# Differential attention block in float32: mask of the scores by VectorE, all modulation rows on TensorE, products begun among them, loads of q and of the output weights moved up

## What is computed

```python
mod = silu(c) @ ada_w + ada_b
shift, scale, gate = split(mod, 3)
h = rms_norm(x, norm_pre) * (1 + scale) + shift
q, k, v, z = (h @ w_in[:, i*2048:(i+1)*2048] for i in range(4))
# per block of 128 queries and head; map m of q, k is [.., m, :]
sc = einsum('qmd,kmd->mqk', q, k) * 128 ** -0.5
mask = key_chunk <= q_chunk                      # chunks of 64
p = softmax(where(mask, sc, -1e30))
attn = p[0] - lam * p[1]
o = rms_norm(attn @ v, subln) * (1 - 0.2) * silu(z)
out = x + gate * rms_norm(o @ w_out, norm_post)
```

## Time and profile before

| | |
|---|---|
| median of 3 runs | 2067.22 us (2063.76 to 2068.3) |
| profiled execution | 2068.47 us |
| its span, first to last instruction | 2066.7 us |
| mean granted TensorE clock | 0.985 |
| TensorE busy | 1981.3 us, 96% |
| VectorE busy | 1295.6 us, 63% |
| ScalarE busy | 785.1 us, 38% |
| GpSimd busy | 580.9 us, 28% |

### The profile page before, as it was taken

How to read it: one execution, slowest core, us unless ns; L and a number is a source line. 1 busy time by engine, 2 the same in 40 slices (tenths; PEclk the granted TensorE clock), 3 DMA queues, 4 the chain that set the end, 5 groups by cost and what they waited for, 6 DMA issues and landing times.

```text
span 2066.7 us, 26660 instructions
## 1 busy us (share of the span) xinstructions
PE 1981.3 (96%) x9324; PEld 1610.8 (78%) x9324; DVE 1295.6 (63%) x1988; ACT 785.1 (38%) x1567; POOL 580.9 (28%) x640
## 2 busy tenths in 40 slices
PE   3689999999999989999999999999999989999998
PEld 1168888888888878788888888888888878888886
DVE  3766676666566436777777777777777745434343
ACT  4333333333454323344444444444444333322240
POOL 2333233233456224232332333233232210000000
PEclk9889999999999999999999999999999999999999
DMA  9657666663556586776758676676767685476552
GB/s 311 198 183 244 221 199 207 200 197 124 175 183 227 211 325 219 207 236 195 233 178 248 196 216 216 209 236 200 234 193 237 196 275 165 123 229 199 178 153 82
DMA packets 391489, 426.52 MB, mean 206 GB/s; under 512 B 21078, under 2 KB 287420, under 8 KB 388796
## 3 DMA queue, kind: packets, MB, share of 16 engines
q1 hardware_dynamic: 391072, 424.76, 65.1%
q10 hardware_dynamic: 284, 0.05, 0.0%
HBM read 294.70 MB, written 130.03 MB: 206 GB/s over the span
## 4 chain that ended last, share of the span: by engine, by line
PE 90%; DMA 2%; DVE 2%; issue 2%; POOL 1%; ACT 1%; SPq 1%; DVEq 0%; POOLq 0%; ACTq 0%
PE ps L1561 28%; PE ps L1563 27%; PE ps L1562 27%; PE ps L1667 2%; PE ps L1675 2%; PE ps L1645 1%; DVE acc L1146 1%; PE ps L1541 1%; SPq L475 1%; PE ps L1694 1%; POOL sums L727 1%; POOL stg L747 1%; DMA h_dr<-stg 1%; DVE blk L1175 0%; DMA w_raw<-in_diff_w_out_dram 0%
## 5 line engine op out<-in xcount | busy, mean ns | idle before, releaser
L1561 PE MATMUL ps<-blk,ring 128*128 128x512 f32 x1536 | 612.4, 399 | 12.6 <-POOL blk L738 5.9
L1563 PE MATMUL ps<-blk,ring 128*128 128x512 f32 x1536 | 600.9, 391 | 0.0
L1562 PE MATMUL ps<-blk,ring 128*128 128x512 f32 x1536 | 600.4, 391 | 0.0
L1561 PEld LDWEIGHTS ps<-blk,ring 128*128 128x128 f32 x1536 | 289.7, 189 | 73.1 <-issue 12.1
L1563 PEld LDWEIGHTS ps<-blk,ring 128*128 128x128 f32 x1536 | 289.5, 188 | 62.2
L1562 PEld LDWEIGHTS ps<-blk,ring 128*128 128x128 f32 x1536 | 290.1, 189 | 57.2
L1111 DVE TENSOR_TENSOR ring<-sums,ring 128x512 fp32r<-128x512 f32 x256 | 221.1, 864 | 128.8 <-ACT ring L830 125.6
L727 POOL TENSOR_TENSOR sums<-raw 128x512 f32<-128x512 f32 x128 | 192.6, 1505 | 307.5 <-DVE ring L1111 290.4
L830 ACT ACTIVATE ring<-sums 128x512 fp32r<-128x512 f32 x256 | 160.4, 627 | 202.3 <-PE ps L1563 195.8
L1111 DVE TENSOR_TENSOR ring<-raw,ring 128x512 fp32r<-128x512 f32 x192 | 162.0, 845 | 83.0 <-ACT ring L830 82.3
L1432 DVE TENSOR_TENSOR w_lo<-w_raw,w_hi 128x512 fp32r<-128x512 f32 x112 | 77.4, 691 | 191.2 <-ACT w_hi L1026 191.1
(11 more groups left out here) (163 smaller groups left out, 3110.1 us busy)
## 6 DMA issues: line engine op xcount, KB each, us to landing
raw<-in_diff_w_in_dram SPq DMA_DIRECT2D x64, 1024.0 KB, 7.0
d_dr<-cc SPq DMA_DIRECT2D x128, 256.0 KB, 2.7
cc<-d_dr SPq DMA_DIRECT2D x128, 256.0 KB, 3.7
w_raw<-in_diff_w_out_dram SPq DMA_DIRECT2D x128, 256.0 KB, 3.6
ada<-in_ada_w_dram SPq DMA_DIRECT2D x108, 256.0 KB, 4.7
ada<-in_ada_w_dram SPq DMA_DIRECT2D x32, 512.0 KB
q_sb<-q_dr SPq DMA_DIRECT2D x64, 256.0 KB, 3.2
k_sb<-k_dr SPq DMA_DIRECT2D x64, 256.0 KB, 3.8
```

The costliest lines, as they stand in the source:

```text
L1561: MM(dst, a_hi, b_hi, start=start, stop=False, skip_group_check=True)
L1562: MM(dst, a_hi, b_lo, start=False, stop=False, skip_group_check=True)
L1563: return MM(dst, a_lo, b_hi, start=False, stop=stop, skip_group_check=True)
```

## The change

1. The mask matmul goes; VectorE writes -1e30 over the corner (64 queries by 64 keys) of the scores, waits for it (`masked`), and takes the maximum.
2. All eight slots of a chunk are TensorE's; `rows0`, `ada_sum` and `acc0` go. The row and its turned columns share one bank, so that a chunk's first row waits for `mod_ok` of the chunk before. All seven low halves are VectorE's.
3. Products 0, 1 and 3 are begun (`begin`) for j = 0 and 1 behind the third chunk, for j = 2 behind the fourth, before its factors are used; only j = 3 is left for `product`. P5 and P3 of the first group use bank 1.
4. SP: the first weight load stands behind slot 7 instead of 15; the first load of q and k ahead of slot NA + 26; the first four loads of the output weights three products before the end of the products; in the last head q and k of the next block behind the first load of a block. ScalarE splits the first output weight before it squares the last block of head 6.

```diff
+    X_BANK = (3, 5, 6, 7)
-    ON_PE = (1, 4, 6, 7)
+    EARLY_PRODUCTS = (0, 1, 3)
...
         def bank_of(i, pi):
+            if i == 0 and pi in (P5, P3):
+                return 1
...
+        LOWS = (0, 1, 3, 2, 4, 5, 6)
+        def start_low(pi):
+            return LOWS.index((P1, P2, P3, P5, P7, P6, P4).index(pi)) + 1
...
                 if s >= ADA_RING:
-                    sp.wait_ge(*slots_of(s - ADA_RING))
+                    sp.wait_ge(ada_used, s - ADA_RING + 1)
...
                 load_ada_start(s)
-                if s == 15:
+                if s == 7:
                     load_raw(0)
...
             for n in range(NA, NA + PARTS_IN * NP):
+                if n == NA + 26:
+                    load_qk(0, 0)
                 slot(n)
-            load_qk(0, 0)
...
                         slot(n)
                         n += 1
+                        if n == NALL - 3:
+                            for j in range(4):
+                                load_wo(j)
                     if a + 1 == LH * NB:
-                        for j in range(4):
-                            load_wo(j)
                         load_oz_first(1, 0)
...
                     if i == 0:
+                        if qb + 1 < NB:
+                            load_qk(LH, qb + 1)
                         if qb == 0:
                             for pi in (P3, P4):
                                 store(2 * GP - 1, pi)
...
                         load_z(LH, qb)
-                        if qb + 1 < NB:
-                            load_qk(LH, qb + 1)
...
-            for j in range(4):
-                if j == 3:
-                    for which in range(4):
-                        add_w(0, which)
-                for y in range(3):
-                    pool.wait_ge(h_hi, j * NP + y + 1)
...
-                    TTP(dst[:, 1, j], src, dst[:, 0, j].bitcast(F32), ALU.subtract).then_inc(h_lo_p, 1)
+            for which in range(4):
+                add_w(0, which)
...
+                modulate(4 * j)
+                high_h(0)
+                modulate(4 * j + 1)
+                modulate(4 * j + 2)
+                high_h(1)
+                modulate(4 * j + 3)
+                for y in range(2, NP):
+                    high_h(y)
...
+                    if a + 1 == LH * NB:
+                        split_next(-1)
                     square(h - 1, qb)
...
-            def rows0(s):
...
+                low_h(0)
+                block_sums(ch, tA, 0)
+                low_h(1)
+                block_sums(ch, tA, 1)
+                low_h(3)
+                block_sums(ch, tA, 2)
+                low_h(2)
+                low_h(4)
+                block_sums(ch, tA, 3)
+                low_h(5)
+                low_h(6)
...
                 dve.wait_ge(s_done, a * 2 + m + 1)
+                V.memset(ps[0:CHUNK, bank + qb // HT, qb % HT * P + CHUNK:(qb % HT + 1) * P], MASKED).then_inc(masked, 1)
+                dve.wait_ge(masked, a * 2 + m + 1)
                 V.tensor_reduce(out=nmax[:, m:m + 1], in_=ps[:, bank:bank + 2].rearrange("p b n -> p (b n)")[:, 0:n],
...
                 pe.wait_ge(ada0_in[s % ADA_RING], 32 * (s // ADA_RING + 1))
+                if r == 0 and ch:
+                    pe.wait_ge(mod_ok, ch)
...
+            def begin(j):
+
+                for pi in EARLY_PRODUCTS:
+                    if j == 0:
+                        pe.wait_ge(w_ok, pi + 1)
+                    pe.wait_ge(h_lo_d, NP * j + start_low(pi))
+                    three(ps[:, bank_of(0, pi)], ring[:, pi, 0, j], ring[:, pi, 1, j],
+                          slotA[pi][:, 0, j], slotA[pi][:, 1, j], j == 0, False)
+
             for ch in range(4):
-                for r in ON_PE:
-                    if r == ON_PE[-1]:
-                        ada_sum(ch)
+                for r in range(8):
                     ada_rows(8 * ch + r)
-                    if r == ON_PE[1] and ch:
+                    if r == 4 and ch:
                         for q in range(4):
                             x_turn(4 * ch + q)
                 mod_turn(ch)
+                if ch == 2:
+                    begin(0)
+                    begin(1)
+            begin(2)
...
+                if n == NP:
+                    pe.wait_ge(*read_out(0, P3))
                 if i == 0:
-                    if pi in (P1, P2, P3):
-                        pe.wait_ge(h_lo_p, 9 + (P1, P2, P3).index(pi) + 1)
-                    else:
-                        pe.wait_ge(h_lo_d, 12 + (P5, P7, P6, P4).index(pi) + 1)
+                    pe.wait_ge(h_lo_d, 3 * NP + start_low(pi))
...
-                for j in range(KB):
+                for j in range(KB - 1 if n in EARLY_PRODUCTS else 0, KB):
...
-                    own = e == n
-                    last = three(dst, q_sb[:, 2 * m], q_sb[:, 2 * m + 1], k_sb[:, 2 * m, b:e], k_sb[:, 2 * m + 1, b:e], True, not own)
-                    if own:
-                        last = MM(ps[:, bank + b // HALF, e - b - P:e - b], mcol[0:1, :], mrow[0:1, :], start=False, stop=True,
-                                  skip_group_check=True)
+                    last = three(dst, q_sb[:, 2 * m], q_sb[:, 2 * m + 1], k_sb[:, 2 * m, b:e], k_sb[:, 2 * m + 1, b:e], True, True)
```

More of the change, by code:

```diff
@@ L862, in modulate, with high_h @@
                 act.wait_ge(xT_mm, y + 1)
[L863 removed]
+                A(h32[:, q // 2, half * HALF:(half + 1) * HALF], ps[:, X_BANK[q] if js < 4 else VX], ACT.Identity,
                   scale=mod[:, KT + k:KT + k + 1], bias=mod[:, k:k + 1]).then_inc(h_ev, 1)
             for j in range(4):
[L867 to L868 removed]
+                if j in (1, 2):
+                    for m in (2 * j - 2, 2 * j - 1):
                         high_w(m)
[L870 to L876 removed]
+                act.wait_ge(ada_used, 8 * (j + 1))
+                A(mod_row[0:1, :], ps[0:1, SC], ACT.Copy).then_inc(mod_row_ok, 1)
+                def high_h(y):
+                    if y < 3:
+                        act.wait_ge(h_ev, 4 * j + (1, 3, 4)[y])
+                    else:
                         act.wait_ge(h_sum, 4 * j + y - 2)
@@ L981, in before, with split_next @@
                 return divmod(a - 1, NB)
+            def split_next(u):
+                n = u + 1
+                if n < REG:
+                    act.wait_ge(wo_in[POS[n] % 4], (POS[n] // 4 + 1) * 16)
+                    if n < 2:
+                        act.wait_ge(prod, NALL - 1)
+                    else:
+                        act.wait_ge(wo_used, n - 1)
+                    A(w_hi[:, n % 2], w_raw[:, POS[n] % 4], ACT.Copy).then_inc(wo_hi_ok, 1)
+                if REG - KT <= n < REG:
+                    m = n + KT
+                    act.wait_ge(wo_in[POS[m] % 4], (POS[m] // 4 + 1) * 16)
+                    if m == REG:
+                        act.wait_ge(fin, HT)
+                    A(wl_hi[:, m - REG].rearrange("p (a c) -> p a c", c=P), w_raw[:, POS[m] % 4],
+                      ACT.Copy).then_inc(wo_hi_ok, 1)
             for n in range(NA, NA + PARTS_IN * NP):
@@ L1134, in _ @@
                 V.tensor_scalar(x1[:, :, t, :], x1[:, :, t, :], rsx[:, t:t + 1], None, ALU.mult).then_inc(x_sc, 1)
-            def rows0(s):
-                ch, r = divmod(s, 8)
-                dve.wait_ge(ada0_in[s % ADA_RING], 32 * (s // ADA_RING + 1))
-                for m in range(2):
-                    done = 8 * ch + 2 * (r - sum(q < r for q in ON_PE)) + m
-                    g = 2 * r + m
-                    if g == 0:
-                        i = V.tensor_scalar(acc0[:, ch % 2], ada_start(s)[:, m], cact[:, g:g + 1], None, ALU.mult)
-                    else:
-                        dve.wait_ge(row_ok, done)
-                        i = STT(acc0[:, ch % 2], ada_start(s)[:, m], cact[:, g:g + 1], acc0[:, ch % 2], ALU.mult, ALU.add)
-                    i.then_inc(row_ok, 1)
-            for r in range(8):
-                if r not in ON_PE:
-                    rows0(r)
             for ch in range(4):
-                if ch < 3:
-                    rows0(8 * ch + 8)
-                if ch == 3:
-                    for m in range(LOOK):
+                if ch in (1, 2):
+                    for m in (2 * ch - 2, 2 * ch - 1):
                         low_w(m)
@@ L1530, in x_turn @@
                 for t in range(HT):
[L1531 removed]
+                    i = TR(ps[:, X_BANK[q] if js < 4 else VX, t * P:(t + 1) * P], src[:, k, half * HT + t], ident[:, :])
                 i.then_inc(xT_mm, 1)
```

111 lines of the change are left out of this document (28 added, 83 removed).

## The result

| | before | after |
|---|---|---|
| median of 4 runs, us | 2067.76 (2063.76 to 2071.16) | 2009.06 (2007.15 to 2010.03) |
| profiled execution, us / its span | 2068.47 / 2066.7 | 2007.15 / 2005.2 |
| ratio, 95% interval | | 0.9723 (0.9704 to 0.9742) |

The change saves 58.7 us by the medians, 61.3 by the profiled executions; forecast were 68, a time of 2000. The direction is right and the size is short by nine: the measured median lies at the upper end of the range (1992 to 2010), and by the ratio (0.9723 x 2067.22) it is 2010.0. Where it went is read from the starts of the 64 turns of prob, which cut the program into stretches.

What follows compares the result with a forecast made beforehand. TensorE, busy for 96% of the span, was taken as the bound; 49.3 - 1 + 5.3 + 2 + 3 + 9.5 = 68.1 us off 2068.5 gave 2000.4, said as 2000. Its own range was 1993 to 2008, with four rivals 1992 to 2010.

Steps and rivals of the forecast that it cites:

- A mask matmul costs 0.44 us of TensorE: In the gapless heads, each of 112 mask matmuls removed saves 0.44 us of TensorE, 49.3 us in all.
- The lower bound, 0.25: Gapless heads: each mask saves only its own slot, 0.25 us (28 us in all); as a rival 2021, chance 0.06.
- The write costs 0.30 with its wait: VectorE's write of the masked corner, done 128 times, takes 0.30 us including the wait for it.
- It comes out 0.13 short; seven heads give 1 us back.: Block 3's turn of prob: margin of 0.37 us falls 0.13 short, so TensorE waits; 1 us lost over seven heads.
- the first rival: VectorE late at more turns, its steps twice as long beside POOL: half a microsecond more in some blocks, 2009; chance 0.12.
- The start, -2: Start, all row matmuls on TensorE and products begun early: product 3 ends at 128.1 instead of 130.0, 2 us gained.
- the rival on the clock: Start: TensorE's clock falls at each chunk, four falls costing 2.2 us each, 2009; chance 0.07.
- q and k of the first block, -3: Before the first scores: earlier loads remove 1.25 us of TensorE idle and 1.7 of slow clock, 3 us.
- The last head's first ticks, -9.5: Start of the last head: earlier output weight and q, k loads recover 9.5 of 3.7 + 6.4 = 10.1 us.
- late again, by other names: Rival on the moved loads: they are late again, all 12.5 us of their gain stay unsaved, 2012.5; chance 0.09.
- Last head's masks, 5.3: Last head: eight masks of map 0 and four of map 1 count, 12 x 0.44 = 5.3 us saved.

Runs made afterwards that it cites:

- e9: Changed kernel with GpSimd's three additions of block 3 put ahead of its factor of block 2: 2006.49 us, ratio 0.9707 to the kernel before.
- e2: Changed kernel with the mask left out altogether, neither VectorE's write nor a matmul: 2008.58 us, ratio 0.9726 to the kernel before.
- second execution: Second profiled execution of the same changed kernel, unaltered, from a later run: span 2008.0 us, that run's median 2011.33 us.
- e6: Changed kernel with the mod rows of chunk 1 summed in another PSUM bank: 2005.59 us, ratio 0.9706 to the kernel before.
- e10: Changed kernel with the edits of e6, e8 and e9, and ScalarE copying product 0 out ahead of its last high half of h: 2000.87 us.
- e4: Changed kernel with the moved loads put back at three places of SP's program: 2018.00 us, ratio 0.9774 to the kernel before.
- e8: Changed kernel with the 1 MB load of low halves put behind the first four output weight loads: 2008.06 us, ratio 0.9719 to the kernel before.
- e1: Kernel before with only the mask moved from TensorE to VectorE: 2019.06 us, ratio 0.9776 to the kernel before.

## Why the prediction was right or wrong

- **A mask matmul costs 0.44 us of TensorE.** Right. In the two heads of e9 in which TensorE waits for nothing, a head is 110.26 and 110.32, 7.0 to 7.1 under the shortest two before (117.29 and 117.36), and 16 x 0.44 is 7.04. The lower bound, 0.25, would have left heads of 113.4. The margins around the mask go with it, and the change of bank, which stayed, is not their cause. The Trainium skill, "TensorEngine Tiling (Array Packing)", Key Properties, says that a change of tiling mode drains TensorE; whether a one-row weight is such a change no run here shows, and the cause of the margins stays open.
- **The write costs 0.30 with its wait.** Too high, it is 0.15, and on the path almost nothing (e2).
- **"It comes out 0.13 short; seven heads give 1 us back."** This step failed, one of the two that make up most of what is missing. The prediction measured VectorE's lateness against the product behind the scores, and took the mask to leave that chain 0.5 us less margin. In block 3 the chain does not come from the scores: it runs from the weighted sum of block 2 over ScalarE's square and GpSimd's factor to three additions and prob, and both masks lay beside it, between the same weighted sum and the turn on TensorE. So all of 2 x 0.44 was lost to it: 0.37 - 0.88 = -0.51, and the wait is 0.49. By the shortest heads of e9 it costs 0.75 a head, 5.3 us instead of 1. e9 removes the wait in every head; its trace gets 2.2 us of the 5.3 back, since the load of cc is late next in five heads.
- **VectorE's steps are twice as long beside GpSimd** stood in the first rival, as a reason why other blocks might be late, with 2009 and a chance of 0.12. The time came out there, but not that way: one block waits four times as long as forecast, a little over half of the rival's nine, and the start and the last head give the rest. That the time is this rival's, and still inside the range, is luck. Block 1 shows the other half: its prob is now held (1.48 for 0.48) and its margin went from 0.74 to 0.15, without a wait.
- **The start, -2.** It gave 0.7, and 1.2 in the second execution, by the start of the last product ahead of the scores. Closing the chunks was costed without the clock: behind chunks 0 and 1 it fell, which cost 0.21 x 8.20 and 0.18 x 9.55, 1.7 us each by the stretches above, and the rows ended at 112.20, not 109.8. This is the rival on the clock, at two chunks of its four; e6 shows it. And product 2 waited 0.6 for ScalarE's copy of product 0, which the prediction did not name (e10).
- **q and k of the first block, -3.** Right, 3.0 in both executions: the last product ahead of them starts 0.7 sooner than before, the first turn behind them 4.6, and 0.9 of that is two masks. More than half of it was the clock: with the loads back (e4) the gap came back and the fall of the clock did not, and it cost 1.5.
- **The last head's first ticks, -9.5.** The other step that failed, short by 3.3 and 6.5 us, which is the largest miss in the second execution: it gave 6.2 in one execution and 3.0 in the other, when 2.2 for five masks is taken off. The late q was SP's order, and moving it helped. SP's order was not what held the output weight (e4): issued 7.4 us ahead of the end of TensorE's work before (1651.17 to 1658.53), and 11.6 ahead now (1597.45 to 1609.03), the first one lands 0.6 us behind that end before and 0.3 now, and its split and the first product follow 1.5 later. What SP issued ahead of it, now:

```profile
1594.94 1.00 SPq L570 DMA_DIRECT2D hT_lo<-oz_dr  x2
1595.99 0.51 SPq L570 DMA_DIRECT2D hT_hi<-oz_dr  x1
...
1597.45 4.37 SPq L562 DMA_DIRECT2D w_raw<-in_diff_w_out_dram  x4
```

Each of the three loads of hT is 1 MB; with q, k, a store of z and the first weight itself some 4 MB were issued in 3.5 us. With 1 MB of them put behind the weights (e8) the first one lands at 1607.20 instead of 1609.33. The price was read from the gap; what bounds the gap was not asked. It is in substance the rival "late again, by other names", at a part of its 12.5 us.
- **Last head's masks, 5.3.** About right: 3.7 where 3.1 were due behind block 2.
- Not forecast: a load that was 0.9 us late in the second head before was not late after. Such gaps come and go (e1 has two, e9 five).

## What to carry to other kernels

A margin at a wait is the margin of one chain. Before counting what an edit takes from it, follow the waiting step back through every engine, and ask of each step that is longer than its kind what it ends with: if it always ends the same distance behind another engine's step, that engine is in the chain. Time taken from the bottleneck is taken from every chain that starts on it, in full. When a wait is gone, read which one comes next (here a load) before the gain is counted. Where a load is late, add up the bytes in flight ahead of it before moving its issue; and of a stretch that depends on loads read two executions.

## What the runs showed of the hardware

- **VectorE and GpSimd exclude each other by whole operations.** In the kernel before, 100 subtractions of two SBUF operands on L1111 began under one of GpSimd's additions (L727) and lasted over 0.95 us, for 0.69 alone. All of them ended 0.55 to 0.56 us after that addition, however early they began; steps on 256 elements ended 0.28 behind, on one element 0.02. The Trainium skill, "SBUF — State Buffer", SBUF: two separate sides, has this: the port pair that the two share is an exclusive lock for the whole instruction, and a VectorE step with two SBUF inputs has to wait while a GpSimd step that reads SBUF holds it. The trace agrees that such a step waits for the addition's end; it then ends 0.14 us sooner than its 0.69 alone would have it. The two held steps of block 3 (1.07 and 1.32 us) were in the trace before; the earlier trace rows shows only prob behind them, which is not held. It goes both ways: the additions that met such steps took 1.56 and 1.74 us, the free one 1.29.
- **DMA engines at a share of 0.98 to 1.05** moved 339 to 380 GB/s between 1597 and 1609 us, around the first output product, in four executions (348 and 365 in the changed kernel, 339 in e2, 380 in e10). "DMA: Bandwidth & Descriptors", Specifications, in the Trainium skill gives about 358 GB/s as the limit of memory for one core; the runs lie around it, two of them above.
- **A gap of 3.3 us in which TensorE worked for 1.05** (49.8 to 53.06) was followed by a stretch partly at half the clock (granted 0.79 over 49.8 to 58 us); where the rows went on right behind the turn (e6) the clock stayed at 1.00. The expectation of e6 put the fall at 5 us of half speed each, 2.5 us lost; by the granted clock 1.7 us were lost at each of the two chunks.
